# The unit stage as a pipeline over three units, each TensorE tile shape once per turn

## The reference

```python
def step(state, inp):
    r_t, w_t, k_t, v_t, a_t, b_t = inp
    sa = jnp.einsum('dbhij,dbhj->dbhi', state, a_t)
    state = (state * w_t[..., None, :] + sa[..., :, None] * b_t[..., None, :]
             + v_t[..., :, None] * k_t[..., None, :])
    y_t = jnp.einsum('dbhij,dbhj->dbhi', state, r_t)
    return state, y_t
...
bonus = jnp.sum(r * k * r_k.astype(f32), axis=-1, keepdims=True) * v
```

## Time and profile before

| | |
|---|---|
| runs | 3551.37, 3552.51, 3554.97 us; median 3552.51 |
| span of the profiled execution | 3551.0 us |
| PE busy | 3364.8 us (95% of the span) |
| PE weight loads busy | 2210.4 us (62%) |
| DVE busy | 2381.0 us (67%) |
| ACT busy | 1465.5 us (41%) |
| POOL busy | 518.6 us (15%) |

### The profile page before, as it was taken

One profiled execution on the slowest core, in us unless ns is written; L12 is line 12 of the kernel. 1 busy time (PEld: TensorE's weight loads), 2 busy tenths in 40 slices (PEclk: granted clock), 3 DMA queues, 4 the chain that ended last, 5 costly groups with the idle time before them and its releaser, 6 DMA issues. The chain is left out here.

```text
span 3551.0 us, 56035 instructions
## 1 busy us (share of the span) xinstructions
PE 3364.8 (95%) x20921; PEld 2210.4 (62%) x20921; DVE 2381.0 (67%) x4134; ACT 1465.5 (41%) x3398; POOL 518.6 (15%) x776
## 2 busy tenths in 40 slices
PE   8999999999999997999999986899999989999998
PEld 6787788444444444888888874567667664444444
DVE  3555554699988972676777766677777777864444
ACT  4445445434434442333333314566666642112222
POOL 1242234200000000222222210000000002222121
PEclk9999999999999998999999998899999999999999
DMA  4443444713124123544434455100000026532121
GB/s 157 142 155 125 137 137 149 249 57 120 61 97 140 66 68 122 152 140 116 120 113 122 115 167 185 53 12 12 12 15 12 13 94 242 171 136 80 54 80 39
DMA packets 312215, 376.25 MB, mean 106 GB/s; under 512 B 121756, under 2 KB 233832, under 8 KB 309552
## 3 DMA queue, kind: packets, MB, share of 16 engines
q1 hardware_dynamic: 298544, 362.66, 31.1%
q10 hardware_dynamic: 13440, 10.49, 0.9%
HBM read 205.31 MB, written 167.77 MB: 105 GB/s over the span
## 5 line engine op out<-in xcount | busy, mean ns | idle before, releaser
L1998 PE MATMUL at_g<-at_kT,at_qz 64*128 64x512 f32 x1088 | 300.8, 634 | 21.4 <-DVEq L1923 16.1
L656 PE MATMUL cv_pj<-u_room,w 128*128 128x257 f32 (+1 forms) x1344 | 302.8, 383 | 3.2 <-ACT cv_zwin L333 1.3
L2023 PEld LDWEIGHTS at_pb<-at_v,at_attT 128*128 128x128 f32 x2176 | 251.4, 193 | 64.6 <-issue 47.0
L656 PEld LDWEIGHTS cv_pj<-u_room,w 128*128 128x128 f32 (+1 forms) x1344 | 246.4, 186 | 58.2 <-issue 18.2
L2023 PE MATMUL at_pb<-at_v,at_attT 128*128 128x128 f32 x2176 | 266.8, 280 | 13.0 <-ACT at_attT L1906 13.0
L1306 DVE TENSOR_TENSOR un_su<-un_sc,corner_room 128x448 f32<-128x448 f32 x320 | 184.8, 619 | 60.0 <-PE un_sc L1372 56.8
L1078 PE MATMUL rs_tm<-w,rs_uT 128*128 128x512 f32 x480 | 207.9, 593 | 3.4 <-ACTq L963 3.4
L1078 PE MATMUL rs_tm<-w,x_pair 128*128 128x512 f32 x416 | 189.0, 614 | 18.3 <-ACTq L963 14.1
L656 PE MATMUL cv_pj<-cv_uT,w 128*128 128x257 f32 (+1 forms) x896 | 200.4, 381 | 0.0
L1906 ACT COPY at_attT<-at_tb 128x512 f32<-128x512 f32 x272 | 147.4, 587 | 117.4 <-PE at_tb L2015 117.2
L1998 PEld LDWEIGHTS at_g<-at_kT,at_qz 64*128 64x128 f32 x1088 | 127.8, 190 | 98.7 <-issue 72.3
(11 more groups left out here) (343 smaller groups left out, 6902.7 us busy)
## 6 DMA issues: line engine op xcount, KB each, us to landing
scratch_packs<-pack_room SPq DMA_DIRECT2D x19, 2048.0 KB, 6.7
pack_room<-scratch_packs SPq DMA_DIRECT2D x54, 640.0 KB, 4.0
un_pk<-scratch_packs SPq DMA_DIRECT2D x26, 640.0 KB, 4.1
w<-in_w_in_dram SPq DMA_DIRECT2D x6, 2048.0 KB, 14.4
scratch_gate<-rs_tok_out SPq DMA_DIRECT2D x40, 256.0 KB, 2.4
scratch_q_kT<-rs_qk_out SPq DMA_DIRECT2D x40, 256.0 KB, 3.4
pack_room<-scratch_tblk SPq DMA_DIRECT2D x160, 64.0 KB, 4.1
scratch_local<-un_local_out SPq DMA_DIRECT2D x80, 128.0 KB, 1.7
```

Of the source, the lines that this page charges most:

```text
L656: last = nc.tensor.matmul(pj[n % 3][0:r, 0:HALF], w[:, c, m * P:m * P + r], uT[b % 2][:, c, HALF * hf:HALF * hf + HALF], start=(c == 0), s ...
L1998: last = nc.tensor.matmul(gb[m][:, c * 512:(c + 1) * 512], qz[par][rows, h, :], kT[rows, h, at:at + 512], start=True, stop=True)
L2023: last = nc.tensor.matmul(pb[h % 2][:, 0:P], attT[h % 2][:, c, :], v[:, c, h * P:(h + 1) * P], start=(c == 0), stop=(c == count - 1))
```

## The change

The unit stage becomes a pipeline over three units. PE's turn n (from -2 to 80) works on n, n+1 and n+2: off blocks of n+1 and joined of n; all scores of n+2; applied of n, inner of n+1, turned of n+2, full outputs of n; half outputs of n. The scores of both directions get a bank pair each (`sc[0]`, `sc[1]`), and the transposes are written into the first pair once its masks are done. `su`, `vz`, `bk_tok`, `ad` and `fp` get a third copy, in memory of the attention phase that is idle here. DVE's turn: sums of n-1 half 0, joined copies of n, off-block copy of n+1, masks of n+2 d = 0, sums of n-1 half 1, masks of n+2 d = 1, inner copy of n+1. The bonus moves from DVE to ACT, with its sums copied out of PSUM first (`bn`). SP loads pack and corners of n+4 as soon as POOL and the turning of n+1, and its off blocks, are done; solved halves have semaphores of their own (`st0` to `st2`). The initial counts that ACT and DVE added to semaphores go, as do the `passed` increments.

```diff
-        su = [ph.sb(f"su{i}", [P, 2, 2, 448]) for i in range(2)]
-        vz = [ph.sb(f"vz{i}", [P, P]) for i in range(2)]
-        bk_tok = [ph.sb(f"bk_tok{i}", [P, 2, 2, P]) for i in range(2)]
+        su = [ph.sb(f"su{i}", [P, 2, 2, 448])[:, :, :, :] for i in range(2)] + [idle.k_room[:, 0:1792].rearrange("p (d h n) -> p d h n", d=2, h=2)]
+        vz = [ph.sb(f"vz{i}", [P, P])[:, :] for i in range(2)] + [idle.v_room[:, 512:640]]
+        bk_tok = [ph.sb(f"bk_tok{i}", [P, 2, 2, P])[:, :, :, :] for i in range(2)] + [idle.v_room[:, 0:512].rearrange("p (k d c) -> p k d c", k=2, d=2)]
...
-        sc = ph.banks("sc", 2)
-        tr = ph.banks("tr", 2)
+        sc = [ph.banks(f"sc{d}", 2) for d in range(2)]
+        tr = sc[0]
...
+            for n in range(NI):
+                if n + 4 < NI:
+                    next_pack(n + 4)
+                    next_corners(n + 4)
                 if n + 3 < NI:
-                    load(n + 3)
-                store(n, n % 2)
+                    sp.wait_ge(s["wz_ready"], n + 1)
+                    ahead.load_solved(sp, n + 3)
+                if n:
+                    store(n - 1)
...
+            def bonus(n):
+                act.wait_ge(s["va_evac"], 4 * n + 4)
                 for h in range(2):
+                    nc.scalar.activation(local_out[n % 3][:, 1, 64 * h:64 * h + 64], vz[n % 3][:, 64 * h:64 * h + 64], ACT.Copy, scale=bn[n % 3][:, h:h + 1]).then_inc(s["bonus_done"], 1)
+
+            for n in turns:
+                if real(n - 1):
+                    y_part(n - 1, 0)
+                    y_part(n - 1, 1)
+                    own(n - 1, 0)
+                if real(n):
+                    joined(n)
+                if real(n - 1):
+                    own(n - 1, 1)
+                    bonus(n - 1)
+                if real(n + 2):
+                    turned(n + 2)
...
+            for n in turns:
+                if real(n - 1):
+                    sums(n - 1, 0)
+                if real(n):
+                    solved(n)
+                if real(n + 1):
+                    off_block(n + 1)
+                if real(n + 2):
+                    masked(n + 2, 0)
+                if real(n - 1):
+                    sums(n - 1, 1)
+                if real(n + 2):
+                    masked(n + 2, 1)
+                if real(n + 1):
+                    inner_part(n + 1)
...
+            for n in turns:
+                if real(n + 1):
+                    off_blocks(n + 1)
+                if real(n):
+                    joined(n)
+                if real(n + 2):
+                    scores(n + 2)
+                if real(n):
+                    applied(n)
+                if real(n + 1):
+                    inner(n + 1)
+                if real(n + 2):
+                    turned(n + 2)
+                if real(n):
+                    full_outputs(n)
+                    half_outputs(n)
```

More of the change, by code:

```diff
@@ L1165, in unit_phase, with real, carry_at, halves @@
         SU_AK, SU_RK, SU_OFF, SU_RB = (0, 128), (128, 0), (256, 384), (320, 256)
[L1167 to L1172, removed]
+        turns = range(-2, NI + 1)
+        def real(n):
+            return 0 <= n < NI
+        def carry_at(n, rows, d, first, last):
             if n < NCH:
-                return carry_out[par][rows, d, first:last]
+                return carry_out[n % 2][rows, d, first:last]
             return kept[rows, n - NCH, d, first:last]
-        def nxt(n, j, par):
-            return n + 1, j + par, 1 - par
+        def halves(h):
+            return slice(64 * h, 64 * h + 64), slice(64 - 64 * h, 128 - 64 * h)
         @block.sync
@@ L1251, in body, with own @@
                                             ALU.mult).then_inc(s["ad_ready"], 1)
-            for n in range(NI):
-                body(n, n // 2, n % 2)
         @block.scalar
         def _(act):
[L1258 to L1263, removed]
-                act.wait_ge(s["va_ready"], n + 1)
-                nc.scalar.copy(vz[par][:, :], tr[0][:, 0:P]).then_inc(s["va_evac"], 1)
+            def own(n, h):
+                hs, ys = halves(h)
+                act.wait_ge(s["carry_evac"], n * 4 + 2 * h + 2)
+                nc.scalar.copy(carry_at(n, hs, slice(0, 2), 192, 256), ob[h][hs, 384:512].rearrange("p (d c) -> p d c", d=2)).then_inc(s["own_evac"], 1)
@@ L1316, in body, with solved @@
[L1316 to L1317 removed]
+                    nc.vector.tensor_tensor(su[n % 3][:, d, h, :], sc[d][h][:, 0:448], mask[:, d, :], ALU.mult).then_inc(s["su_done"], 1)
+            def solved(n):
                 dve.wait_ge(s["q_ready"], n + 1)
@@ L1374, in turned, with off_blocks @@
-            def turned(n, j, par):
+            def off_blocks(n):
+                pe.wait_ge(s["su_done"], 4 * n + 4)
+                pe.wait_ge(s[f"tf{n % 3}"], n // 3 * 32 + 32)
+                if n:
+                    pe.wait_ge(s["xf_evac"], n)
+                    pe.wait_ge(s["x_evac"], n)
+                for h in range(2):
+                    for d in range(2):
+                        r, e = slice(64 * d, 64 * d + 64), slice(64 - 64 * d, 128 - 64 * d)
+                        last = mm(xq[e, 256 + 64 * h:320 + 64 * h], su[n % 3][r, d, h, SU_OFF[d]:SU_OFF[d] + 64], tf[n % 3][r, h, :], start=True, stop=True)
+                last.then_inc(s["xf_ready"], 1)
@@ new lines, in joined @@
+            def joined(n):
+                pe.wait_ge(s["xf_evac"], n + 1)
+                pe.wait_ge(s["x_evac"], n + 1)
+                pe.wait_ge(s[f"st{n % 3}"], n // 3 * 32 + 32)
+                if n:
+                    pe.wait_ge(s["q_evac"], 2 * n)
+                for h in range(2):
+                    for d in range(2):
+                        r, e = slice(64 * d, 64 * d + 64), slice(64 - 64 * d, 128 - 64 * d)
+                        last = mm(xq[r, 384 + 64 * h:448 + 64 * h], xf[n % 2][e, h, :], tt[n % 3][e, 2 * d + h, e], start=True, stop=True)
+                last.then_inc(s["q_ready"], 1)
@@ new lines, in scores @@
+            def scores(n):
+                p_ = pk[n % 3]
+                pe.wait_ge(s[f"in{n % 3}"], n // 3 * 16 + 16)
+                if n:
+                    pe.wait_ge(s["va_evac"], 4 * n)
+                    pe.wait_ge(s["bk_evac"], n)
+                    pe.wait_ge(s["su_done"], 4 * n)
+                for d in range(2):
+                    ar = PK_AR + 256 * d
+                    off = ar + 64 if d == 0 else ar
+                    b_at = PK_BK + 256 * d
+                    for h in range(2):
+                        hs, ys = halves(h)
+                        mm(sc[d][h][:, 256:448], p_[hs, b_at:b_at + P], p_[hs, off:off + 192], start=True, stop=True)
+                    for h in range(2):
+                        hs, ys = halves(h)
+                        mm(sc[d][h][:, 0:256], p_[hs, b_at + P:b_at + 256], p_[hs, ar:ar + 256], start=True, stop=True).then_inc(s["sc_ready"], 1)
@@ new lines, in applied @@
+            def applied(n):
+                pe.wait_ge(s["q_evac"], 2 * n + 2)
+                pe.wait_ge(s["x_evac"], n + 1)
+                pe.wait_ge(s["va_evac"], 4 * n + 3)
+                if n:
+                    pe.wait_ge(s["wz_evac"], n)
+                for d in range(2):
+                    for h in range(2):
+                        u = 2 * d + h
+                        last = mm(wb[:, P * u:P * u + P], tt[n % 3][:, u, :], ax[n % 2][:, d, h, :], start=True, stop=True)
+                last.then_inc(s["wz_ready"], 1)
@@ new lines, in inner @@
+            def inner(n):
+                pe.wait_ge(s["su_done"], 4 * n + 4)
+                pe.wait_ge(s["va_evac"], 4 * n + 1)
+                pe.wait_ge(s["xf_evac"], n + 1)
+                if n:
+                    pe.wait_ge(s["q_evac"], 2 * n)
+                    pe.wait_ge(s["x_evac"], n)
+                for d in range(2):
+                    for h in range(2):
+                        last = mm(xq[:, 128 * d + 64 * h:128 * d + 64 * h + 64], su[n % 3][:, d, h, SU_AK[d]:SU_AK[d] + P], vz[n % 3][:, 64 * h:64 * h + 64], start=True, stop=True)
+                last.then_inc(s["x_ready"], 1)
@@ L1450, in outputs @@
-                for d in range(2):
-                    for h in range(2):
-                        last = into(ob[h][:, 192 * d:192 * d + P], wz[par][:, d, h, :], su[par][:, d, h, SU_RB[d]:SU_RB[d] + P])
-                        if d:
-                            last.then_inc(s["out_ready"], 1)
-            scores(0, 0, 0, 0)
-            turned(0, 0, 0)
-            scores(0, 0, 0, 1)
-            inner(0, 0)
-            def body(n, j, par, more):
-                m, jm, pm = nxt(n, j, par)
-                if more:
-                    scores(m, jm, pm, 0)
-                    turned(m, jm, pm)
-                joined(n, par)
-                if more:
-                    scores(m, jm, pm, 1)
-                applied(n, par)
-                if more:
-                    inner(m, pm)
-                outputs(n, par)
@@ L2557, in hybrid_encoder @@
```

(2 more changed lines are left out.)

258 lines of the change are left out of this document (101 added, 157 removed).

## The result

After 3466.36 us (median of 4 runs, 3465.8 to 3468.61), before 3551.94 on the same chip: ratio 0.9759, interval 0.9745 to 0.9773. The forecast was 3471. The page of the kernel after, beside the earlier trace rows: its first line, PE's and DVE's busy time, the granted clock.

What follows compares the result with a forecast made beforehand. PE's work was taken to bound the stage; a turn falls from 8.53 to 7.45 us, and with fill and drain the net is -80.7: 3552.5 - 80.7 = 3471.8, stated as 3471, range 3460 to 3484 (78 in 100).

Steps and rivals of the forecast that it cites:

- PE's turn: PE in the unit stage: work 6.80 us plus four shape changes at 0.165, walked to 7.45 us against 8.53.
- Rival A: At PE's joints: overhead belongs to a block's head with its waits, not its shape; 3524 us; 5 in 100.
- The stall: PE between applied and inner: the 0.41 us wait goes, since inner reads masks made a turn earlier.
- The margins: PE's waits in the new turn: room of 0.38 us at applied, 0.64 turned, 0.52 full outputs, 1.25 next off-blocks.
- Rival B: A new PE wait ends last, DVE or ACT 0.4 to 0.9 us later; 3495, up to 3530; 10 in 100.
- ScalarE: ACT in the new turn: two scalings 0.25 us each, narrow copy 0.2; from 2.6 to 3.3 us a turn.
- Fill and drain: Stage's ends: two partly slow filling turns, turn 0 +1.5 us, last two turns 6.2 each, bonus after last copy +0.5.
- The cited rules: On PE: the bank rule would give some 3507 us, the weight-load rule 3524; neither entered the sum.
- C: DVE becomes the ring's bound; slower from 1.4 times longer instructions, 3608 us at 1.5 times; 3 in 100.
- D: Removed shape changes are worth more (0.20) and fewer fill turns are slow: 3455 to 3462 us; 4 in 100.

Runs made afterwards that it cites:

- e1: c1 with the scores of n+2 cut in two, d=1 behind applied (two more shape changes between row tiles): 3496.84 us, ratio 0.9844.
- e3: Kernel after with two long-satisfied waits in the middle of each of PE's eight blocks, 16 more a turn: 3465.31 us, ratio 0.9752.
- e9: Kernel before with inner and off blocks reading the other unit's masks, and DVE's half-1 sums ahead of the d=1 masks: 3517.84 us, ratio 0.9908.
- c1: Kernel after with DVE's joined copies of n put before the half-0 sums of n-1: 3481.7 us, ratio 0.981.
- e4: Kernel after with the bonus back on DVE, behind the half-1 sums, and taken from ScalarE: 3465.3 us, ratio 0.9757.
- e5: Kernel after with the bonus on DVE, done twice, ahead of the joined copies: 3496.91 us, ratio 0.9845.
- e6: Kernel before with inner and off blocks reading the other unit's masks, so not waiting for their own last mask: 3541.18 us, ratio 0.997.
- e10: Kernel after with the bonus on DVE, done twice, just ahead of the half-1 sums: 3486.57 us, ratio 0.9813.

## Why the prediction was right, step by step

**PE's turn.** Right to 0.02 us. The work is what the spacings gave, and a change of shape costs what its joint showed in the earlier trace rows. The experiments price it without the walk: 0.195 (rows), 0.17 (columns), 0.17 as the mean of four removed. Rival A's ground, that nearly every change stood at a wait, is gone with e1 and e3. One place within the turn was walked wrongly: inner begins 1.00 us after applied, not 0.90. In the first 128*128 block behind a change of shape the second matmul comes 0.1 us later than the spacing inside a block (0.21 for 0.11 us at applied); the prediction left that at the end of the joined 128*128 blocks, and it falls behind the first matmul of applied. It does not change the sum (3.82 for the four blocks, 3.86 walked).

**The stall.** The 0.41 went, but "the 0.41 goes, since inner(n+1) now reads masks made a turn earlier" names half the reason. Alone that is worth 0.13; the other 0.28 to 0.29 needed sums ahead of masks d=1 as well, which the new order also has. The prediction did not give that as a reason, so here it was lucky. Rival A's turn of 8.12, the one with this gain alone, took two edits to reach (8.11 in e9): 3551.0 - 3517.8 = 33.2 us, the 3551.0 being the kernel before on the same chip. From there to after it is some 51 us, the changes of shape with fill and drain.

**The margins.** At applied 0.38 was walked; the copies end 1.82 into the turn and the load is at 2.32, 0.45 with DVE's 0.05. At full outputs the walk took the sums, 4.57 against 5.09, margin 0.52. The sums end at 4.43, but what ends last there is ScalarE's own copy, 4.42 + 0.22 = 4.64 against the load at 5.05 (unrounded times): 0.41. This step was mis-sized without effect on the forecast, and it is why c1 was missed: its 0.62 passes 0.41 by 0.21, which is what the turn grew by. Rival B was thus nearer than written, one order of DVE away.

**ScalarE.** The two scalings take 0.59 (0.5 taken), the narrow copy 0.19 (0.2). The DVE time saved was worth nothing, as said (e4).

**Fill and drain.** The time is 4.6 us below 3471, and the fill, with turn 0, gave most of it. First load to the last off blocks: 596.4 forecast, 591.4 measured. The fill gave 2.1 of these 5.0 (turn 0 starts 11.7 us after the first load, not 13.8), turn 0 another 1.1 (it took 7.89 us, not 8.95; its scores wait until 0.22 us after ScalarE's last turning copy), and the 77 full turns 1.8. The last two turns took 6.53 each, not 6.2. PE in the first of them, then PE in the second with what ends before its load:

```profile
1980.16 1.16 PE L1427 MATMUL un_wb<-un_ax,pack_room 128*128 128x128 f32 x8 [1.19 <-DVE pack_room L1328]
...
1982.47 1.13 PE L1458 MATMUL un_ob<-un_su,un_wz 128*128 128x128 f32 x8 [0.32 <-ACT kept L1267]
...
1989.01 1.13 PE L1458 MATMUL un_ob<-un_su,un_wz 128*128 128x128 f32 x8 [1.16 <-ACT kept L1267]
```

```profile
1987.34 0.28 DVE L1353 TENSOR_TENSOR un_local_out<-un_ob,un_local_out 64x128 f32<-64x128 f32 x1
1988.50 0.26 ACT L1267 COPY kept<-un_ob 64x128 f32<-64x128 f32 x1
1988.98 0.97 PEld L1458 LDWEIGHTS un_ob<-un_su,un_wz 128*128 128x128 f32 x8 [1.32 <-ACT un_wz L1281]
```

With no scores to cover them, both the copies and ScalarE's own copy are waited for, and the latter was left out of the walk. Here DVE's sums end at 1987.62, over 1.3 us before the load, so what the load follows by 0.22 is ScalarE's copy (1988.76). The tail grew by 0.8 (5.96 against 5.13 from the last matmul's end), not 0.5. Together -80.7 - 5.0 + 0.7 + 0.3 = -84.7; measured -84.6.

**The cited rules.** By the rule of the Trainium skill (TensorEngine Tiling (Array Packing), Restrictions and Gotchas, Gotcha 1: PSUM Pressure) that different row tiles can't use one PSUM bank at once, the run would have been some 3507. The trace contradicts it here: L1385 and L1397 still run in pairs, eight matmuls in 0.45 and 0.40 us. By the rule of the Trainium skill (TensorE: Matmul & The Clock Gate, Part 3) that weight loads overlap running matmuls only where the row group differs, the 128*128 blocks would have stayed apart. The trace contradicts that as well: inner's first matmul follows applied's last by 0.11 us, less than the 0.275 us of one of them.

C (DVE bound) did not come up: DVE is busy 423.17 of 574 us. Of D, the shorter fill came true, the dearer changes did not.

## What to carry to other kernels

Count the changes of tile shape in a TensorE loop and price one at its joint. Putting blocks of one shape from several independent units side by side turns that into time, if each block has its inputs a turn early. Before a stall is booked as gain, look for the next wait behind it whose source is queued behind the first one's: here two thirds of a stall were covered by it. When you walk a margin, end it on every engine that signals, each with its own lag, and walk the order of the queues too: one exchange in DVE's order cost 15 us.

## What was unexpected of the hardware

- A weight load follows VectorE's recorded end by 0.05 us (mask 1657.69 to load 1657.74 in before; e5) and ScalarE's by 0.22 (c1, e6, e10, and without a rival in the last turns: 1988.50 + 0.26 = 1988.76, load 1988.98). Such a wait stands as "issue" or under another engine in the views. Whether it is the signal or the write that takes longer, no run tells.
- Sixteen satisfied waits a turn on PE cost nothing measurable.
- The product with two columns takes about 0.2 us on PE (1655.68 to 1655.87 in after), nearly twice a 128-column transpose (0.109); replacing it by one was worth 0.11 a turn.
- Four 128x64 scalings on DVE took 0.78 us, though two by themselves read 0.42: within a run of them one follows the other about 0.16 us after its start.
